# A hybrid attention and mLSTM layer on one Trainium2 core: the mLSTM projections as five Strassen passes over pairs of tiles, in one stage with the last five

## The reference

```python
h = rmsnorm(x, g_pre); p = h @ w_in + b_in
# columns of p: q_a k_a v_a z_a | q_m k_m v_m o_m z_m | i_m f_m | g_a g_b
y_a = attn(q_a, k_a, v_a) * silu(z_a)            # window 128, 16 meta keys, sinks, rotary
y_m = sigmoid(o_m) * mlstm(q_m, k_m, v_m, i_m, f_m) * silu(z_m)   # 4 heads of width 256
merged = sigmoid(g_a) * (y_a @ w_pa) + sigmoid(g_b) * (y_m @ w_pb)
x = x + rmsnorm(merged @ w_out, g_post)
# mLSTM, per chunk of 128 rows and per head, state C (256 x 256) and n (256):
#   Wqk = W * (q k^T);  num = a * (q C) + Wqk v;  den = a * (q n) + rowsum(Wqk)
#   h = num / max(|den|, exp(-m));  C = aL * C + (k * wL)^T v;  n = aL * n + sum(k * wL)
```

## Time and profile before

| | us |
|---|---|
| median of 3 runs | 2902.96 |
| span of the profiled execution | 2898.6 |
| TensorE busy | 2829.1 (98%) |
| VectorE busy | 1503.2 (52%) |
| ScalarE busy | 1023.7 (35%) |
| GpSimd busy | 1441.1 (50%) |
| last weighted sum of the attention ends | 837.3 |
| mLSTM stage, first to last matmul | 845.3 to 2051.2 |
| last five passes, first to last matmul | 2052.9 to 2888.9 |

### The profile page before, as it was taken

The page is one execution under the profiler, slowest core; times in us unless marked ns, Lnnn a source line. Parts: engine busy times, 40 slices in busy tenths (PEclk is TensorE's granted clock), DMA queues, the critical chain, the costliest instruction groups (busy, mean ns, idle before and its releaser), DMA issues. The chain is left out here.

```text
span 2898.6 us, 49203 instructions
## 1 busy us (share of the span) xinstructions
PE 2829.1 (98%) x16916; PEld 2411.7 (83%) x16916; DVE 1503.2 (52%) x3813; ACT 1023.7 (35%) x2367; POOL 1441.1 (50%) x1638
## 2 busy tenths in 40 slices
PE   6999999999999999999999999999999999999998
PEld 5888888888878888788878887888788888878887
DVE  5776665556533335333533344333555655566687
ACT  5775544445441113112312122111333323333443
POOL 3335534534444555545545554553554544456576
PEclk9999999999999999999999999999999999999999
DMA  7432212222236533654354544643728574485843
GB/s 261 146 128 83 80 59 96 73 79 92 81 114 212 172 131 122 225 175 141 131 189 158 183 138 136 224 156 113 249 102 310 205 276 181 164 336 193 316 175 131
DMA packets 206777, 473.73 MB, mean 163 GB/s; under 512 B 20930, under 2 KB 76231, under 8 KB 202676
## 3 DMA queue, kind: packets, MB, share of 16 engines
q1 hardware_dynamic: 187028, 408.86, 41.1%
q10 hardware_dynamic: 16800, 52.54, 4.9%
q0 software_dynamic: 2720, 9.32, 1.0%
HBM read 316.24 MB, written 156.38 MB: 163 GB/s over the span
## 5 line engine op out<-in xcount | busy, mean ns | idle before, releaser
L311 POOL TENSOR_TENSOR a_all<-h_raw,a_all 128x256 fp32r<-128x256 f32 x548 | 397.8, 757 | 631.7 <-issue 445.4
L321 PE MATMUL bank_first<-w_all,a_all 128*128 128x384 f32 (+1 forms) x1088 | 415.3, 382 | 3.2 <-POOL a_all L311 2.3
L323 PE MATMUL bank_first<-w_all,a_all 128*128 128x384 f32 (+1 forms) x1088 | 394.5, 363 | 0.0
L322 PE MATMUL bank_first<-w_all,a_all 128*128 128x384 f32 (+1 forms) x1088 | 394.4, 362 | 0.0
L584 ACT ACTIVATE ml_qkt<-ml_pt 128x512 f32<-128x512 f32 x68 | 40.7, 598 | 903.6 <-PE ml_pt L890 903.6
L2614 DVE TENSOR_TENSOR a_all<-sums,a_all 128x512 fp32r<-128x512 f32 x163 | 178.3, 1095 | 163.7 <-ACT a_all L2488 162.5
L321 PEld LDWEIGHTS bank_first<-w_all,a_all 128*128 128x128 f32 x1088 | 204.5, 188 | 50.7 <-issue 27.1
L709 DVE TENSOR_TENSOR ml_qk<-bank_first,bias_all 128x512 f32<-128x512 f32 x66 | 45.7, 692 | 370.5 <-ACT ml_kw L588 370.5
L323 PEld LDWEIGHTS bank_first<-w_all,a_all 128*128 128x128 f32 x1088 | 204.4, 188 | 22.2
L321 PE MATMUL bank_second<-w_all,a_all 128*128 128x512 f32 x544 | 220.1, 405 | 2.3 <-ACT w_all L198 1.5
L322 PEld LDWEIGHTS bank_first<-w_all,a_all 128*128 128x128 f32 x1088 | 204.7, 188 | 20.1
(11 more groups left out here) (517 smaller groups left out, 7665.7 us busy)
## 6 DMA issues: line engine op xcount, KB each, us to landing
w_split<-w_early SPq DMA_DIRECT2D x140, 512.0 KB, 3.1
h_raw<-h_t SPq DMA_DIRECT2D x121, 512.0 KB, 4.5
w_all<-w_split SPq DMA_DIRECT2D x34, 1024.0 KB, 14.2
stage<-l_chunks_in SPq DMA_DIRECT2D x45, 512.0 KB, 6.8
w_rest<-w_split SPq DMA_DIRECT2D x16, 1024.0 KB, 10.1
w_early<-w_split SPq DMA_DIRECT2D x14, 1024.0 KB, 7.5
w_plain<-l_x_t_in SPq DMA_DIRECT2D x17, 512.0 KB, 4.9
h_t<-h_raw SPq DMA_DIRECT2D x17, 512.0 KB, 5.7
```

Source lines behind the costliest of these rows:

```text
L311: q = nc.gpsimd.tensor_tensor(k.h_lo[:, u, j:j + 2], k.h_raw[:, u, j:j + 2], k.h_hi[:, u, j:j + 2].bitcast(F32), ALU.subtract)
L321: nc.tensor.matmul(out, hi[:, j], k.w_hi[:, j, col:col + n], start=(j == 0), stop=False)
L322: nc.tensor.matmul(out, hi[:, j], k.w_lo[:, j, col:col + n], start=False, stop=False)
L323: last = nc.tensor.matmul(out, lo[:, j], k.w_hi[:, j, col:col + n], start=False, stop=(j == KT - 1))
```

## The change

Three things change.

1. The stages mLSTM and tail become one, `stream`, of ten passes: ZM, H0 to H3, GA, PA, GB, PB, OUT. ZM makes the columns z of all heads and stores them in HBM; H0 to H3 make q, k, o and v of one head each, 1024 columns. All ten use the seven-product scheme, with tile 0 first and the eight pairs after it. In the seven streamed passes (ZM, H0 to H3, GA, GB) the operands, sums included, come ready from HBM, 256 KB for each product. The mLSTM steps of a tile stand between products: the transposes after one product, the score after the next, the mixing and the state products after the one behind. The sample products of tile 0 stand inside products, between matmuls. There is one bank each for x, y and z; four of the others serve the mLSTM.
2. The weights come to SBUF unsplit. A pass has 28 units of 128 x 512; each is loaded into one of six waiting slots, ScalarE makes its high part and GpSimd its low part (VectorE for 6 of 28), two units per product, from six products ahead of the pass to its eighth.
3. The attention stage makes the operand sums of the row pairs (s_t) and the differences of the weight blocks of all ten passes (difs_t), on GpSimd, 80 times four subtractions of 128 x 256, loaded and stored by SP. It no longer projects the first mLSTM tile; in its last pass it splits the first 16 units.

The parts of the diff of which the text speaks, cut to their core:

```diff
-POOL_CHUNKS = (6, 7)
+N_PASS = 10
+ZM, H0, H1, H2, H3, GA, PA, GB, PB, OUT = range(N_PASS)
+STREAMED = (ZM, H0, H1, H2, H3, GA, GB)
+NEEDED = (T3, B22, B11, B21, T1, T2, T4)
+N_UNIT = 4 * len(NEEDED)
+EARLY = 16
+N_DIF = 2 * KH * N_PASS
...
+def turned_at(n):
+    h, t = n // NT, n % NT
+    b = N_PROD * (H0 + h)
+    if t < 3:
+        return b + (6, 13, 16)[t]
+    return b + N_SINGLE + N_PAIR * ((t + 1) // 2) + (0 if t % 2 else 3)
+def scored_at(n):
+    return turned_at(n) + 1
+def mixed_at(n):
+    return turned_at(n) + 2
+SAMPLE = {mixed_at(NT * h): h for h in range(MH)}
+UPDATE = {mixed_at(NT * h) + 1 + x: (h, x) for h in range(MH) for x in range(4)}
+def lower_by_dve(v):
+    s, block, kt = v // N_UNIT, v % N_UNIT // KH, v % KH
+    return s > 0 and block in (2, 3, 5) and kt % 2 == 1
+def unit_split_at(v):
+    s, x = v // N_UNIT, v % N_UNIT
+    if s == 0:
+        return -3 if x < EARLY + KH else (x - EARLY - KH) // 2
+    return N_PROD * s - 6 + x // 2
```

TensorE, inside `product(q)` and after it:

```diff
+                new = i == 0 or i == 1 and block_used in (T1, T2, T4)
                 for t in range(KH):
-                    hi, lo = a_part(q, 0)[:, t, :], a_part(q, 1)[:, t, :]
-                    T.matmul(bank_of(bank, at), hi, w_row(at, 0, t), start=fresh and t == 0, stop=False,
+                    if new:
+                        wait_unit(pe, N_UNIT * s + KH * NEEDED.index(block_used) + t)
+                    for i in (2 * t - 4, 2 * t - 3) if q in SAMPLE and t >= 2 else ():
+                        sample_rows(SAMPLE[q], i)
+                    if q in UPDATE and t % 2 == 0:
+                        state_update(UPDATE[q][0], 2 * UPDATE[q][1] + t // 2)
+                    hi, lo = k.a_all[:, 0, q % NA, t, :], k.a_all[:, 1, q % NA, t, :]
+                    T.matmul(bank_view(bank, at), hi, weight_row(k, at, 0, t), start=fresh and t == 0, stop=False,
                              skip_group_check=True)
...
+            def state_update(h, i):
...
+                elif i == 1:
+                    pe.wait_ge(c_ready, n + 1)
+                else:
+                    pe.wait_ge(cs_ready, JD * NB * h + 2 * (i - 1))
...
             for q in range(Q_ALL):
-                if q > 1:
-                    product(q)
+                product(q)
+                if q in MIX:
+                    mix(MIX[q])
+                if q in META:
+                    meta_state(META[q])
+                if q in TURN:
+                    turn(TURN[q])
+                if q in SCORE:
+                    if SCORE[q]:
+                        y_transposed(SCORE[q] - 1)
+                    score(SCORE[q])
```

VectorE, in the order of its queue (in step q it has waited for the end of product q - 1):

```diff
+            for q in range(-3, Q_ALL + 8):
+                if 0 < q <= Q_ALL:
...
+                        dve.wait_ge(prod, q)
+                        if i:
+                            evict_pair(g, j)
...
+                if q + 3 < Q_ALL:
+                    split_operand(q + 3)
...
+                n = MIX.get(q - 1)
+                if n is not None:
+                    outputs(n)
+                if q - 1 in UPDATE:
+                    sample_states(*UPDATE[q - 1])
...
+                for v in SPLITS_AT.get(q, ()) if q >= 0 else ():
+                    if lower_by_dve(v):
+                        lower_unit(v)
```

GpSimd in the stream, and its new work in the attention:

```diff
+            for q in range(Q_ALL + 8):
+                if 0 < q <= Q_ALL:
...
+                    if i and j == P6:
+                        second_sums(g)
+                    if i and j == P7:
+                        last_sum(g)
...
+                        finish(g, row)
...
+                        if j == (1 if i else 0):
+                            make_sums(g, 0)
+                        if j == (4 if i else 2):
+                            make_sums(g, 1)
+                for v in SPLITS_AT.get(q, ()):
+                    if not lower_by_dve(v):
+                        lower_unit(v)
...
+        def difs_by(m):
+            return max(0, m - 2) if m <= 2 * NT else min(N_DIF, 2 * NT - 2 + (m - 2 * NT) * 3 // 2)
...
+            def differences(c):
+                G, d = nc.gpsimd, dif[dif_buffer(c)]
+                pool.wait_ge(dif_in[dif_buffer(c)], 16 * (dif_turn(c) + 1))
+                G.tensor_tensor(d[:, R11], d[:, R12], d[:, R11], ALU.subtract).then_inc(dif_step, 1)
...
```

The SP queue loads a unit one product ahead of its split, once the unit six before it has its low part:

```diff
+            def load_unit(v):
+                if v - NW >= EARLY:
+                    wait_unit(sp, v - NW)
+                sp.dma_start(waiting[:, (v - EARLY) % NW], unit_source(k, v)).then_inc(unit_in[(v - EARLY) % NW], 16)
```

More of the change, by code:

```diff
@@ L1276, in _ @@
                 sp.wait_ge(o, 16 * KVH * NT // 2)
+            for i in range(3):
+                sp.wait_ge(dif_out[i], 16 * sum(dif_buffer(c) == i for c in range(N_DIF)))
         @block.gpsimd
@@ L2157, in tail, with line_of, row_turn, stored_count @@
-def tail(nc, k):
+    i = g % N_ITEM
+    return (2 * i - 1, 2 * i) if i else (0,)
+def line_of(g, row):
+    return 2 if is_single(g) else row
+def row_turn(passes, g, row):
+    return (N_ITEM - row) * passes.index(g // N_ITEM) + g % N_ITEM + 1 - row
+def stored_count(g):
+    n = STORING.index(g // N_ITEM)
+    return 16 * (n + 1 if is_single(g) else (N_ITEM - 1) * n + g % N_ITEM)
+def former_item(g, row):
+    h = g - N_ITEM if is_single(g) else (g - 2 if is_single(g - 1) else g - 1)
+    return h if h >= 0 and row < len(tile_rows(h)) else None
@@ L2226, in operand, with wait_raw @@
+        def wait_raw(eng, g):
+            eng.wait_ge(raw_in[summed_number(g) % 2], 16 * (summed_number(g) // 2 + 1))
+        def operand(q):
+            s, i, j = place(q)
+            g = N_ITEM * s + i
+            if s in STREAMED:
+                return sums[:, q % NA]
             if is_single(g):
@@ L2250, in stored, with negated @@
[L2250 to L2273 removed]
+        def negated(q):
+            return q % N_PROD == 0
@@ new lines, in wait_whole, with begun, ended @@
+        def wait_whole(eng, g, row):
+            if row:
+                eng.wait_ge(c21_ready, pairs_before(g) + 1)
+                eng.wait_ge(c22_ready, pairs_before(g) + 1)
+            else:
+                eng.wait_ge(c11_ready, g + 1)
+                eng.wait_ge(c12_ready, g + 1)
+        def begun(q):
+            g = begins(q)
+            return g if g is not None and g < G_ALL else None
+        def ended(q, row):
+            g = begins(q)
+            return g - 1 if g and row < len(tile_rows(g - 1)) else None
@@ new lines, in _ @@
+                g = ended(q - 1, 1)
+                if g is not None and g // N_ITEM in (PA, PB):
+                    wait_whole(dve, g, 1)
+                    scale_row(g, 1, slice(0, D))
+                for row in range(2):
+                    g = ended(q - 1 - 2 * row, row)
+                    if g is not None and g // N_ITEM == OUT:
+                        norm_row(g, row)
+                for v in SPLITS_AT.get(q, ()) if q >= 0 else ():
+                    if lower_by_dve(v):
+                        lower_unit(v)
@@ new lines, in state_update @@
+            def state_update(h, i):
+                n = NT * h
+                if i == 0:
+                    pe.wait_ge(n_done, n + 1)
+                    pe.wait_ge(kwz_ready, NB // 2 * (h + 1))
+                    pe.wait_ge(qkt_ready, n + 1)
+                    pe.wait_ge(wqk_ready, n + 1)
+                    if n:
+                        pe.wait_ge(yt_ready, n)
+                elif i == 1:
+                    pe.wait_ge(c_ready, n + 1)
+                else:
+                    pe.wait_ge(cs_ready, JD * NB * h + 2 * (i - 1))
+                for part in range(2):
+                    b, j = i // JD + part * NB // 2, i % JD
+                    T.matmul(update_bank(i, part)[:, 0:MD + 1], kwz[sample_rows_of(b), b % (NB // 2), j * P:(j + 1) * P],
+                             vaug(n)[sample_rows_of(b)], start=True, stop=True).then_inc(us_done, 1)
@@ L2789, in _ @@
                 for row in range(2):
-                    g = begins(q - 1 - 2 * row)
-                    if g and row < len(tile_rows(g - 1)) and (g - 1) // N_ITEM == PB:
-                        transposes(g - 1, row)
+                    g = ended(q - 1 - 2 * row, row)
+                    if g is not None and g // N_ITEM == PB:
+                        transposes(g, row)
 def hybrid_layer(nc, k):
```

2014 lines of the change are left out of this document (909 added, 1105 removed).

## The result

The changed kernel took **3156.2 us** in the median of four runs (3148.78 to 3160.51), the kernel before 2903.27. The ratio is 1.087, 95% interval 1.085 to 1.089: 8.7% slower, where 0.8% faster was forecast. The profiled execution spans 3158.7 us.

The account below looks back on a forecast made before the run. TensorE was taken to bound the kernel. A bare sum of 2788.7 us plus 30, 38, 3 and 15 gave a 2874.7 us span; with 4.4 for the median, 2879 us, 0.8% faster, range 2820 to 2938.

Parts of the forecast that it names:

- The first stage: Attention stage: GpSimd's added work delays VectorE by 0.23 us per step, 15 us in all; GpSimd meets its due times.
- TensorE needs 7200 x 0.2267: Stream: 7200 matmuls at the 2.4 GHz pace, plus 274 and 21.3 us of other TensorE work, 1927.5 us.
- three of 2.5 us per head: Head passes: TensorE waits for VectorE's sample state updates, three times 2.5 us in each of four heads, 30 us.
- They are the same instructions after: mLSTM in the stream: transposes, scores, mixing and state products keep their 274 us on TensorE.
- 21.3 us of PB: PB's transposes and small waits, 21.3 us of the old tail, carry over unchanged.
- The boundaries of PA, PB and OUT: Starts of these passes: TensorE waits for GpSimd's lower halves, 7, 10 and 21 us, together 38.
- 3 for all the streamed passes: Boundaries of passes with streamed operands: ScalarE and the DMA queue run late by about 2 us; 3 us for all.
- The 119 us of matmuls: TensorE's projections: 119 us go, 109 by seven products for eight and 10 by wider matmuls.
- The slower one (2): Rival: in the attention, the differences delay VectorE's chain by 1 us per step, giving 2928 us; chance 0.13.
- (1): Rival: GpSimd has room, so boundaries and first stage cost nothing, giving 2823 us; chance 0.15.
- (3): Rival: under contention GpSimd's instructions take 1.73 us instead of 1.45, boundaries cost more, giving 2907 us; chance 0.07.
- (4): Rival: the change issues as many matmuls as before, 109 us more, giving 2988 us; chance 0.01.

Follow-up runs that it names:

- tuned: Changed kernel, nothing left out: sums moved off the h buffers, differences split between attention and heads, stream work reordered; 2878.2 us, ratio 0.9915 to the kernel before.
- no_differences: Changed kernel without the differences of the weights, their loads and stores, reading plain blocks instead; 3068.3 us.
- neither: Changed kernel without both the operand sums and the differences of the weights; 2968.2 us.

## Why the prediction was wrong

**The first stage was the step that failed: 15 us, measured 175.** The prediction took a price for each step from GpSimd's busy time ("8 to 11 us of each") and from VectorE's slack, and said that GpSimd "still meets its own due times". It did not follow what the operand sums do to the two buffers of h: which transfer may start only when they are done (the load of the next tile), what it takes (5.4 us from its issue to the split), and who stands behind its reader (the exponentials, on ScalarE's queue). The sums were counted as 33 instructions; their price was the chain, 112 us in steps 15 to 34 with the clock that fell behind its gaps. The steps with two differences and early units were too full by 5 to 7 us each; a mean over 64 steps hid them. The cost to VectorE, which the prediction looked at instead, is real but small: 9.4 us over steps 1 to 14, that is 0.8 in each of steps 3 to 13, and nothing in the later steps with one difference. TensorE's waits in steps 1 to 14 name VectorE, and they go with the differences:

```profile
PE at_bank_pt L1330 <- DVE h_raw L998: 9.9, 11, 0.9
```

In the stream the same VectorE split takes 0.69 us at rest and, in several places, 1.74 to 1.79 beside GpSimd's unit splits, for instance:

```profile
1469.60 1.79 DVE L2376 TENSOR_TENSOR a_all<-h_raw,a_all 128x512 fp32r<-128x512 f32 x1
...
1469.58 1.27 POOL L2068 TENSOR_TENSOR w_all<-st_waiting,w_all 128x512 fp32r<-128x512 f32 x1 [1.24 <-ACT w_all L2207]
```

By the Trainium skill (page SBUF — State Buffer, section SBUF: two separate sides) the engine that comes second is blocked for the whole instruction, which agrees; but at its worst the rule would have cost the attention more than the gain of the change, and it cost 0.8 us per step at most. The measurement decides.

**The clock was left out of the sum.** "TensorE needs 7200 x 0.2267" priced every matmul of the stream at 2.4 GHz, because the earlier trace rows showed 0.99 to 1.00. That kernel had few gaps; the prediction itself added three of 2.5 us per head and priced them at their own length. The mechanism and the length were right (three per head, 2.38 us against 2.5, the sample updates as releaser); undoing them gave 69.9 us in the heads, more than twice the waits. The Trainium skill's page TensorE: Matmul & The Clock Gate (section Wait — 56ns, not 53.3ns?) gives 426.7 ns from start to start at 512 columns at the lower level; the trace has 0.427, three steps in 1.28 us:

```profile
1506.42 0.63 PE L2662 MATMUL bank_second<-w_all,a_all 128*128 128x512 f32 x1
...
1507.70 0.63 PE L2662 MATMUL bank_second<-w_all,a_all 128*128 128x512 f32 x1
```

**"They are the same instructions after" (274 us) and the 21.3 us of PB that "carry over"** were right for the instructions, but missed two reordered waits: PB's transposes stand closer behind the merge than before (25.0 us of waits, 1.5 before), and a head's first tile meets the unit splits of the boundary (16.5 us). The first, before:

```profile
PE tl_bank_t L2724 <- POOL tl_c L2428: 1.5, 1, 1.5
```

**The boundaries of PA, PB and OUT were forecast too dear: 38 us, measured 14.** From GA on TensorE waits 14 us for GpSimd's lower halves. The longest of these waits is in OUT, as forecast, but it is 5.9 us and not 21. The heads have 2.4 us more, against 3 for all the streamed passes. From GA on, the two largest groups:

```profile
PE bank_second L2659 <- POOL w_early L2068: 6.8, 3, 3.1
PE bank_second L2659 <- POOL w_all L2068: 6.6, 2, 5.9
```

OUT took 184.6 us, 21.4 more than its 720 matmuls, which looks like the forecast of 21 and is not: its waits are 11.9 us, half of them for the merge of PB's last rows, and the rest is mostly the clock. PA's 21.6 us hold 12.7 of waits, 5.6 of them for an eviction on ScalarE that was not foreseen and 4.7 for lower halves (7 forecast). The splits for which 1.45 us had been taken lasted 1.46 and 1.51 us in the mean over the whole stream (they answer to the second row), so the price of one was right. Which part of the queue was counted too long stays open.

```profile
L2068 POOL TENSOR_TENSOR w_all<-st_waiting,w_all 128x512 fp32r<-128x512 f32 x154 | 229.0, 1509 | 81.2 <-ACT w_all L2207 81.2
...
L2068 POOL TENSOR_TENSOR w_early<-st_waiting,w_early 128x512 fp32r<-128x512 f32 x56 | 80.7, 1462 | 34.8 <-ACT w_early L2207 34.1 <-DVE a_all L2376 0.6
```

**The 119 us of matmuls were right**: 7200 of them at 0.2267 us are in the trace, and with the faults mended the change is a gain. That tuned, at 2878.2 us, lies 1 us from the forecast of 2879 is a coincidence: it is another kernel, with other waits and, by the estimate above, 17 us of clock.

**The rivals.** The slower one (2) named the right stage and the wrong mechanism: VectorE held up 1 us per step gives 2928, and it was 0.8 in 11 steps. Of (1) it is true that the boundaries cost less than forecast, and untrue that the first stage costs nothing. (3) and (4) did not come about: the splits took 1.46 to 1.51 us, not 1.73, and the matmuls are 7200. Missing was a rival about the load of the h tile, with which every step's work begins, and one about the clock.

Two slips in the sums change nothing: 837.3 + 14 is 851.3 and not 851.5, and the terms of rival (3) give 2904 and not 2907.

## What to carry to other kernels

Work that reads or overwrites a streaming buffer is priced by when the buffer comes free for its next load and by what stands behind the load's reader, not by its own instructions; look first whether it can run on copies of its own. Price a new gap of TensorE at its length and then at half the clock for what follows: here 31 us of waits cost 70. Spread added work by the fullest step, not by the mean, and place it where the queue that issues its transfers has nothing urgent behind it.

## What the runs showed of the hardware that was not expected

Three gaps of 2.38 us, 7 to 10 us from one to the next, in a section where TensorE otherwise works without a break, went with matmuls at half the clock in 19 of the 24 head passes that have them (granted clock 0.54 over 30 us in most, 0.60 or 0.72 in the others) and left five at 1.00, at the same gaps. With the gaps gone, the clock stayed at 1.00 over that section in all 24 head passes of six executions; falls of 3 to 7 us remain elsewhere in some of them. That the same gaps can have either outcome means that a single execution does not price them: no_differences and neither came out 20 and 14 us shorter in the heads, nearly all of it for this.

GpSimd's work beside a busy VectorE was cheaper than feared: 51 jobs of four subtractions (0.74 to 0.76 us each in the attention) made the four head passes 9 us longer in all.
